# Attention of block 1 reordered: stick-breaking first, its mask by TensorE, up-projections by halves, selection rounds among the softmax heads

## What is computed

```python
(c_q, c_kv, k_rope, dq, dk, dv, iq, ik, iw, sq, sk, sv) = jnp.split(proj, offsets, axis=-1)
q = (rms_norm(c_q, mla_q_norm[i]) @ mla_w_uq[i])   # 6 MLA heads of 64 + 32 (rotary)
kv = (rms_norm(c_kv, mla_kv_norm[i]) @ mla_w_ukv[i])
s = einsum(mla_q, mla_k) * 96 ** -0.5; o_mla = softmax(where(causal, s)) @ mla_v
ilog = einsum(idx_q, idx_k) * IDX_DIM ** -0.5
isc = einsum(relu(ilog), idx_w)                    # 8 index heads, summed
_, sel = lax.top_k(isc, topk)                      # 64 of at most 256 keys per query
o_dsa = softmax(dsa_q @ kg + bias) @ vg            # 5 heads over the selected keys
z = einsum(sb_q, sb_k) * SB_DIM ** -0.5            # 5 stick-breaking heads
l1m = where(m, log_sigmoid(-z), 0); suffix = cumsum(l1m, reverse=True) - l1m
w = where(m, exp(log_sigmoid(z) + suffix), 0); o_sb = w @ sb_v      # m: strictly causal
h = h + concatenate([o_mla, o_dsa, o_sb]) @ w_o[i]
```

## Time and profile before

| | us |
|---|---|
| runs | 1634.23, 1616.0, 1617.82 (median 1617.82) |
| the profiled execution | 1622.2, its span 1620.4 |
| TensorE busy | 1470.7 (91%) |
| VectorE busy | 912.0 (56%) |
| ScalarE busy | 679.5 (42%) |
| GpSimd busy | 155.1 (10%) |
| chain that ended last | PE 79%, DVE 13%, issue 3%, ACT 3% |
| attention of block 1, layer 0 (27.9 to 208.4) | 180.5 |
| attention of block 1, layer 1 (457.6 to 619.3) | 161.7 |

### The profile page before, as it was taken

How to read it: one execution, slowest core, us unless ns; L and a number is a source line. 1 busy time by engine, 2 the same in 40 slices (tenths; PEclk the granted TensorE clock), 3 DMA queues, 4 the chain that set the end, 5 groups by cost and what they waited for, 6 DMA issues and landing times.

```text
span 1620.4 us, 24381 instructions
## 1 busy us (share of the span) xinstructions
PE 1470.7 (91%) x10258; PEld 1379.2 (85%) x10258; DVE 912.0 (56%) x1244; ACT 679.5 (42%) x957; POOL 155.1 (10%) x146
## 2 busy tenths in 40 slices
PE   7987999999889699999998959899999469899998
PEld 6977999999889689999986748899998458799997
DVE  5475355555656656555567563554565557365554
ACT  4442254334544435443356333344454224244442
POOL 2000010000110011000022100201021100010000
PEclk9996799999999899999999978899999579799999
DMA  8620145555453134555444431355545210045652
GB/s 233 181 104 1 59 147 192 191 176 183 126 153 143 53 112 162 190 183 196 174 142 154 153 109 53 130 172 192 175 164 189 104 52 2 1 152 186 197 174 98
DMA packets 159656, 225.09 MB, mean 139 GB/s; under 512 B 20105, under 2 KB 126601, under 8 KB 159548
## 3 DMA queue, kind: packets, MB, share of 16 engines
q1 hardware_dynamic: 159548, 223.55, 41.7%
HBM read 222.44 MB, written 1.09 MB: 138 GB/s over the span
## 4 chain that ended last, share of the span: by engine, by line
PE 79%; DVE 13%; issue 3%; ACT 3%; POOL 1%; DMA 0%; DVEq 0%; ACTq 0%; SPq 0%; POOLq 0%
PE ps L1932 16%; PE ps L1933 15%; PE ps L1934 15%; PE ps L1924 4%; PE ps L1925 4%; PE ps L1926 4%; DVE w_lo L1155 3%; PE ps L2162 3%; DVE xT L1179 3%; PE ps L2211 2%; PE ps L2212 2%; PE ps L2213 2%; PE ps L2172 2%; ACT w_hi L710 2%; DVE h L1194 1%
## 5 line engine op out<-in xcount | busy, mean ns | idle before, releaser
L1155 DVE TENSOR_TENSOR w_lo<-raw,w_hi 128x2048 fp32r<-128x2048 f32 (+4 forms) x209 | 476.9, 2288 | 294.1 <-ACT w_hi L710 291.5
L710 ACT ACTIVATE w_hi<-raw 128x2048 fp32r<-128x2048 f32 (+4 forms) x209 | 391.9, 1879 | 233.4 <-PE ps L1934 117.0
L1932 PE MATMUL ps<-xT,w_hi 128*128 128x256 f32 x1600 | 460.0, 287 | 14.9 <-DVE w_lo L1155 13.7
L1933 PE MATMUL ps<-xT,w_hi 128*128 128x256 f32 x1600 | 457.1, 286 | 0.0
L1934 PE MATMUL ps<-xT,w_lo 128*128 128x256 f32 x1600 | 456.9, 286 | 0.0
L1932 PEld LDWEIGHTS ps<-xT,w_hi 128*128 128x128 f32 x1600 | 311.9, 195 | 17.4 <-DVE w_lo L1155 14.9
L1933 PEld LDWEIGHTS ps<-xT,w_hi 128*128 128x128 f32 x1600 | 311.6, 195 | 0.6
L1934 PEld LDWEIGHTS ps<-xT,w_lo 128*128 128x128 f32 x1600 | 311.6, 195 | 0.0
L1932 PE MATMUL ps<-hT,w_hi 128*128 128x256 f32 x640 | 182.3, 285 | 4.6 <-DVE hT L1569 4.6
L1933 PE MATMUL ps<-hT,w_hi 128*128 128x256 f32 x640 | 182.1, 284 | 0.0
L1934 PE MATMUL ps<-hT,w_lo 128*128 128x256 f32 x640 | 182.0, 284 | 0.0
(11 more groups left out here) (290 smaller groups left out, 2097.9 us busy)
## 6 DMA issues: line engine op xcount, KB each, us to landing
raw<-in_w_up_dram SPq DMA_DIRECT2D x54, 1024.0 KB, 5.4
raw<-in_w_down_dram SPq DMA_DIRECT2D x54, 1024.0 KB, 4.9
raw<-in_w_gate_dram SPq DMA_DIRECT2D x22, 1024.0 KB, 5.2
raw<-in_w_in_dram SPq DMA_DIRECT2D x14, 1024.0 KB, 5.8
raw<-in_a_w_in_dram SPq DMA_DIRECT2D x10, 1024.0 KB, 5.1
raw<-in_w_o_dram SPq DMA_DIRECT2D x8, 1024.0 KB, 4.8
raw<-in_w_ple_gate_dram SPq DMA_DIRECT2D x8, 1024.0 KB, 4.8
raw<-in_w_out_dram SPq DMA_DIRECT2D x8, 1024.0 KB, 4.8
```

The lines of the kernel that those rows point to most:

```text
L710: nc.scalar.activation(w_hi[:, p % RH, 0:piece_width(p)], raw[:, p % RR, 0:piece_width(p)], ACT.Copy).then_inc(E["hi_ready"], 1)
L1155: nc.vector.tensor_tensor(w_lo[:, p % RH, 0:w], raw[:, p % RR, 0:w], w_hi[:, p % RH, 0:w].bitcast(F32), ALU.subtract).then_inc(E["lo_ready ...
L1932: nc.tensor.matmul(out_, w[0][:, kk, c], x(0, k), start=start and j == 0, stop=False, skip_group_check=True)
L1933: nc.tensor.matmul(out_, w[0][:, kk, c], x(1, k), start=False, stop=False, skip_group_check=True)
```

## The change

- The pieces come as tok, sq, sk, s4, iq, ikdk, cq, ckv, uq, ukv, dq, w_o; the four pieces of w_o in the order 3, 0, 1, 2 (`W_O`), and the ring's places follow.
- Stick-breaking's first scores lie between the blocks of iq, its second scores between later blocks, each followed by an index score. The index scores go to ps6 and ps7, their relu to `Tsel`.
- The mask is added by TensorE: ScalarE copies the mask and the unit matrix into a place of the ring, and each `stick_z` has two more matmuls of 128x128 (L2356, L2357), 20 in a layer. `stick_sums` and one multiplication on VectorE are gone; ScalarE takes the exponential from PSUM.
- The up-projections go by halves (`lora_half`), each into its own pair of banks.
- Of the eight selection rounds, two follow the stick-breaking outputs, two more stand just ahead of the heads, and one stands in each of the first four heads.
- The heads are a function of their own, with one bank for scores (ps0), one for transposes (ps2) and one for outputs (ps3). The outputs are transposed in pairs of blocks (`turned_pair`, L2547, to ps1): stick-breaking's ahead of the heads, one before head 7's scores, one before the last head is finished, one inside the output product, which starts behind the last values.

```diff
-        add(("w_o", l), tall("w_o", l, KD))
+        add(("w_o", l), [sub("w_o", l, 2 * i, 2, (0, D)) for i in W_O])
...
             def stick_logs(i):
                 dve.wait_ge(E["sb_r"], n["B"] + SB_H)
                 dve.wait_ge(E["sb_l"], n["B"] + i + 1)
-                link(nc.vector.tensor_tensor(sbN[i], sbN[i], sbL[i], ALU.add))
-                nc.vector.tensor_tensor(sbN[i], sbN[i], negm, ALU.mult).then_inc(E["sb_nl"], 1)
-
-            def stick_sums(i):
-                dve.wait_ge(E["sb_s"], n["B"] + i + 1)
-                nc.vector.scalar_tensor_tensor(sbL[i], PS[i % 2][:, 0:384], HD ** -0.5, smask,
-                                               op0=ALU.mult, op1=ALU.add).then_inc(E["sb_w"], 1)
+                nc.vector.scalar_tensor_tensor(sbN[i], sbL[i], -HD ** 0.5, sbN[i], op0=ALU.mult, op1=ALU.add
+                                               ).then_inc(E["sb_nl"], 1)
...
-                select(5 if l == 0 else 4)
-                selected()
-                outputs([MIX_SB + HD * a for a in range(4)], n["O"], None)
-                outputs([MIX_SB + HD * 4], n["O"] + 4, None)
...
+                index_mask()
+                outputs([MIX_SB + HD * a for a in range(4)], n["O"], None, bank=1)
+                outputs([MIX_SB + HD * 4], n["O"] + 4, None, bank=0)
                 cat(l, 1)
...
+                select(2)
+                rest_pair(6)
+                cat(l, 3)
+                used(("dq", l))
+                two_along(allT[:, B_DQ:B_DQ + 2, :], 4)
+                cat(l, 5)
+                select(2)
+                logits(0)
+                for i in range(4):
+                    logits(i + 1)
+                    select(1)
+                    move_pT(i)
+                selected()
...
-            def stick_z(i):
+            def stick_z(l, i):
...
+                mask, ident_r = mask_at(l)
+                nc.tensor.matmul(bank[:, 0:S], allT[r, k, 0:P], allT[r, q, :], start=True, stop=False, skip_group_check=True)
+                nc.tensor.matmul(bank[:, S:384], allT[r, k, P:S], allT[r, q, P:S], start=False, stop=False,
+                                 skip_group_check=True)
+                nc.tensor.matmul(bank[:, 0:P], ident_r, mask, start=False, stop=True, skip_group_check=True)
+                return nc.tensor.matmul(bank[:, S:384], ident_r, mask, start=False, stop=True, skip_group_check=True)
...
                 p = at("dq")
                 pe.wait_ge(E["lo_ready"], p + 1)
+                pe.wait_ge(E["ukv_a"], 2 * l + 1)
+                pe.wait_ge(E["ukv_d"], 2 * l + 1)
+                row_block(p, x, PS[4], 0, 0)
                 pe.wait_ge(E["rope_ready"], l + 1)
+                pe.wait_ge(E["ix_r"], n["X"])
                 cat(l, 0)
+                pe.wait_ge(E["ukv_a"], 2 * l + 2)
+                pe.wait_ge(E["ukv_d"], 2 * l + 2)
                 cat(l, 1)
...
+                pe.wait_ge(E["o_evac"], n["G"])
+                turned_pair(6)
+                row_block(p, x, PS[4], 1, P).then_inc(E["piece_used"], 1)
+                for c in range(2, len(CATS)):
+                    cat(l, c)
...
+                scores(0)
+                pe.wait_ge(E["rt_d"], 6 * l + 6)
+                for i in range(NJ):
+                    if i == 6:
+                        pe.wait_ge(E["o_evac"], G0 + 1)
+                        turned_pair(0)
+                    if i == NJ - 1:
+                        pe.wait_ge(E["o_evac"], G0 + 2)
+                        turned_pair(2)
+                    if i + 1 < NJ:
+                        scores(i + 1)
+                    transposes(i)
+                    if i:
+                        values(i - 1)
+                values(NJ - 1)
+                out_rows(0, 0, 2 * KD)
+                out_rows(1, 0, 2 * KD)
+                out_rows(2, 0, 9)
+                pe.wait_ge(E["o_evac"], G0 + 3)
+                turned_pair(4)
+                out_rows(2, 9, 2 * KD)
...
-                attention(mla_jobs() + dsa_jobs())
-                pe.wait_ge(E["o_evac"], n["G"])
-                to_T(KD, xs, wait_xs=False)
-                tall_product(("w_o", l), ("o", l), 4)
+                heads(l)
```

More of the change, by code:

```diff
@@ L88, in ffn_order @@
     return out + [down[-1]]
+W_O = (3, 0, 1, 2)
 def plan():
@@ L160, in place @@
 def place(use, k):
+    if use[0] == "o":
+        k = 2 * W_O.index(k // 2) + k % 2
     return (KD * USES.index(use) + k) % XR
@@ L496, in bass_two_blocks, with mask_at @@
         B_IQ, B_IK, B_DK, B_SQ, B_SK, B_S4, B_K4, B_DQ = 0, 4, 5, 6, 8, 10, 11, 12
-        CATS = [(src, dst, a) for src, dst in ((qcat, qT), (kcat, kT)) for a in range(0, MLA_H, 2)]
+        CATS = [(src, dst, a) for a in range(0, MLA_H, 2) for src, dst in ((qcat, qT), (kcat, kT))]
+        NJ = MLA_H + DSA_H
+        def mask_at(l):
+            two = xT[:, 0, place(("o", l), 2 * W_O[0]), :]
+            return two[:, 0:P], two[:, P:2 * P]
         def o_before(head0, i):
@@ L768, in mixing @@
                 m = NORM["attn", l] % 2
-                first, behind = FIRST["tok", l], FIRST["iq", l]
+                first, behind = FIRST["tok", l], FIRST["sq", l]
                 for p in range(first, behind):
@@ L1251, in wide_evac, with outputs @@
                     n["wide"] += 1
-            def outputs(dsts, J0, factor, gated=None):
+            def outputs(dsts, J0, factor, gated=None, bank=None):
                 G = n["G"]
@@ L2068, in lora_product @@
                     for t in range(NT):
-                        for half in range(2):
-                            i = by_tokens(PS[base + 2 * t + half][:, 0:w], hidden, k0 + k, t, ws, k, w * half,
-                                          w * half + w, k == 0, k == kn - 1)
-                i.then_inc(E["piece_used"], 1)
+                        i = by_tokens(PS[base + t][:, 0:w], hidden, k0 + k, t, ws, k, w * half, w * half + w,
+                                      k == 0, k == kn - 1)
+                return i
             def mlp(stage, name, blocks, gated):
@@ new lines, in mixing, with flip_ @@
+                pe.wait_ge(E["dkk_ready"], l + 1)
+                for t in range(NT):
+                    i = nc.tensor.transpose(PS[2][:, P * t:P * t + P], kdd[:, t, :], ident)
+                i.then_inc(E["dk_t"], 1)
+                row_block(p, x, PS[4], 0, P).then_inc(E["piece_used"], 1)
+                def flip_(j):
+                    if l == 0:
+                        if j:
+                            pe.wait_ge(E["toep_ready"], j)
+                        nc.tensor.matmul(PS[3][:, :], flip, Tdsa[:, 2 * j:2 * j + 2, :], start=True, stop=True
+                                         ).then_inc(E["flipped"], 1)
```

593 lines of the change are left out of this document (354 added, 239 removed).

## The result

The changed kernel took 1639.65 us (median of 17 runs, 1636.79 to 1677.08), the kernel before 1618.09 in the same comparison (17 runs, 1616.0 to 1638.35). The ratio is 1.010, with a 95% interval of 1.0069 to 1.0132: slower, by less than 2%. Forecast was 1624 in 1594 to 1640, so the time lies just inside the range, and about three times as far from the kernel before as forecast. The profiled execution has a span of 1636.2 us against 1620.4, 15.8 more.

What follows compares the result with a forecast made beforehand. TensorE bounds mixing, VectorE's chain the wait ahead of the heads, the clock the heads. At half clock layer 0 gives -6.2 and layer 1 +11.7, together +5.5 on 1617.8: 1623.3, say 1624 us; range 1594 to 1640.

Steps and rivals of the forecast that it cites:

- the zone: From the last index score to the first head's logits: VectorE chain of 22.9 us, TensorE idle 8.9 of it in pieces.
- D: Rival, mixing: mask products and changes between kinds of product at their upper ends, +9 us, 1633; chance 0.10.
- E: Rival, ahead of the heads: VectorE's chain only moves and nothing is saved, +15 us, 1639; chance 0.05.
- the +5.3: Mixing: TensorE work added per layer, in us, by overlap lost, mask matmuls and going between kinds of product.
- the lost overlap: Mixing: paired stick-breaking scores that ran together now run apart, three times 0.85, 2.6 us a layer.
- the changes of kind: Mixing: going between index-score and stick-breaking products and other blocks, some ten more places, 1.5 us a layer (0 to 3).
- the row block as nearest row: Mixing: a mask matmul priced from a row block's 128x256 matmul (0.12 to 0.13 us), taken as 0.07, upper end 0.22.
- -5.9: Layer 1, up to the end of the first logits: 564.9 instead of 570.8, 5.9 us earlier.
- 41.0: Heads, first logits to output product at half clock: 41.0 us, against 39.9 (layer 0) and 25.4 (layer 1) before.
- A: Rival, heads: full clock comes back or never falls in one layer; 1609, or 1617 if midway; chance 0.27.
- C: Rival, heads: single banks make one serial chain, 5.4 instead of 3.2 us a head, 1671 (over 1650); chance 0.04.
- B: Rival, heads: both layers at full clock, -23.5 us, 1594; chance 0.09.

Runs made afterwards that it cites:

- e8: The changed kernel without the 20 mask matmuls of a layer; 1633.22 us, one run.
- e5: The changed kernel with unused matmuls in TensorE's waits ahead of the heads and also within the heads; 1606.97 us, ratio to the kernel before 0.990.
- e11: e5 with two score banks and two transposed banks instead of one each; 1604.35 us, one run.
- e3: The changed kernel with two score banks and two transposed banks again, as in the kernel before; 1636.01 us, ratio to the kernel before 1.003.
- e2: The kernel before with unused matmuls (62 and 52) in TensorE's one long wait ahead of the heads; 1603.94 us, ratio 0.987.
- e7: e2 with unused matmuls also ahead of two places in mixing where stick-breaking's scores wait; 1598.87 us, ratio to the kernel before 0.985.
- e6: e1 with the four selection rounds moved from the first four heads to ahead of the first logits, 60 filling matmuls there; 1623.85 us, ratio 1.000.
- e1: The changed kernel with 26, 20 and 12 unused matmuls in three TensorE waits ahead of and within the first head; 1623.0 us, ratio to before 0.999.
- e9: e5 with three more unused matmuls ahead of each of four groups of the norms' one-column products in mixing; 1610.37 us, one run.
- e4: The changed kernel without the four selection rounds among the first four heads; 1634.71 us, ratio to the kernel before 1.008.
- e10: e7 with 9 more unused matmuls ahead of the turn and 34 ahead of layer 1's first mixing block; 1601.08 us, ratio to before 0.988.

## Why the prediction was right, and where it was off

**What bounds it** held: mixing is TensorE's, the zone VectorE's, the heads the clock's. The number held by little: 1639.65 against an upper end of 1640, with +5.5 us forecast and +15.8 in the traces. That it fell inside is luck, since the upper end was set by rivals D (1633) and E (1639), and what used that room was neither of them but the clock outside the heads.

**Mixing.** The last index score was to end at 113.1 and ended at 113.3 in layer 0. From the first block that is 86.0 us, not 85.2, so the +5.3 (its terms as written add to 5.5, 20 x 0.07 being 1.4) should have been 6.1 if the work before was 92.5, and its terms were off both ways: a mask matmul costs 0.135 us (e8), not 0.07, 2.7 a layer, and with 2.6 for the lost overlap some 0.8 are left for the changes of kind, not 1.5. The choice of the row block as nearest row was the weak one; between 0.06 and 0.22 the middle, 0.14, was true. No wait for stick-breaking's second scores is left.

**The wait zone.** In layer 0 the first logits were to end 108.1 us after the first block; they end 108.5 after it. The idle pieces were to be 0.4, 3.1, 2.9 and 2.5; they are 0.25, 3.45, 2.85 and 1.81. The chain added up from rows of VectorE came within a microsecond: 22.9 forecast, 22.6 measured.

**Layer 1's mixing is the step that failed.** -5.9 was forecast ahead of the logits, -1.5 measured. The chain of the zone is as long as in layer 0; of the 4.4 missing, 4.2 are clock:

```profile
451.60:457.80 6.20, 6.17 (x29) 6.17 (x30) 4.38 (x2) 0.00 (x0) 0.57 (x1) 0.50 0.85 270
517.00:522.70 5.70, 5.70 (x45) 5.46 (x43) 2.01 (x6) 0.11 (x1) 1.25 (x6) 1.00 0.48 187
522.70:529.50 6.80, 6.80 (x25) 5.93 (x25) 1.49 (x4) 1.69 (x4) 1.24 (x3) 0.50 0.00 0
```

The opening cost 3.1, not 2.3, and 6.8 us at half clock in the middle of mixing cost 3.4, with TensorE never idle in them or in the 5.70 us ahead. The working had taken the half-clock stretches of mixing before away with the waits and put nothing in their place. But the trace of the kernel before already had one that stands behind no wait, in layer 0:

```profile
68.00:73.20 5.20, 5.20 (x42) 4.89 (x41) 2.68 (x7) 2.02 (x2) 0.00 (x0) 1.00 0.45 151
73.20:76.60 3.40, 3.40 (x17) 3.40 (x17) 1.63 (x2) 0.00 (x0) 1.27 (x6) 0.50 0.20 23
```

**The heads.** 41.0 from first logits to product forecast, 41.3 measured in both layers (41.9 from the logits' start). Two of its terms were off and made up for each other: the output bank's two waits took 1.5 us, not 2.4, and VectorE's row made TensorE wait 2.3, not 1.5. The clock was at 0.50 in both, as taken. At full clock 28.0 was worked out for the changed heads; e5 measured 29.0, of which 1.6 is the single banks (e11).

**The product.** +2.0 a layer forecast, +2.2 and +3.3 measured; in layer 1 a second stretch at half clock lies in it (clock 0.92 against 1.00).

**Outside the change** nothing was forecast, and 4.0 us came. Its half-clock stretches are longer by 10 us in all, which would account for up to 5. Over all kernels of the table this unchanged rest takes 806.2 to 813.0 us. It was put at nothing without a reason given.

The sum: layer 0 -5.3 (-6.2 forecast), layer 1 +17.7 (+11.7), the rest +4.0 (0), and 0.6 us less before the first block: +15.8. The mechanism was right in the heads; the mis-sized term is the clock outside them: 4.2 ahead of layer 1's logits, 1.3 in its product and 4.0 in the rest, 9.5 of the 10.3 us that the forecast was short in the traces.

**The rivals.** A did not come by itself. C was excluded by e3. D was half true: the mask 2.7 instead of 1.3, the changes of kind, by the sum above, less. E did not come. B, both layers at full clock, was to give 1594. Made by filling, it gave layer 0 -21.6 (-20.7 worked out) and layer 1 +2.9 (-2.8), 1607 (e5). The forecast for B compared it with the kernel before at its own clock, and that is no fair comparison: filled too, the kernel before has 1604 (e2) and 1599 (e7).

**At equal clock, then, where did the gain go?** e7 against e5, without the half-clock stretches that each still has in this part (6.9 us in e7's layer 0, 6.8 in e5's layer 1, at half their length; the opening of layer 1 is in both): first logits at 110.7 and 108.6 in e7, at 107.9 and 107.3 in e5. So the new order does bring them forward, by 2.8 and 1.3 us. The heads give 3.7 and 4.0 back (29.0 against 25.3 and 25.0, and those have a short stretch at half clock at their turn): 4.6 for the rounds among the first four (e6), 1.6 for the single banks (e11). Splitting the rounds hides little when the clock is full, 1.2 of 5.8 us, since there VectorE bounds the first four heads, and adding the mask takes 4 us of the engine that bounds mixing. In the traces e5 is 7.9 us behind e7, and only 3.6 of that lie in the two layers' attention; 4.1 are in the unchanged rest, which the new order need not have caused. Without the mask products (e8) and with two banks (e11) it might come out ahead; the two together were not run.

**The clock and its rules.** With the long waits ahead of the heads filled, the half clock behind them was gone (e2: 40.6 to 25.3 us in layer 0). The Trainium skill, "TensorE: Matmul & The Clock Gate", section "HAM oscillation", says that waits between bursts of work drop the clock again and that the cost is paid anew each time; for these waits the traces agree. In e1 the clock also fell with waits of only 1.10 and 1.08 us, inside a stretch where TensorE was busy 2.68 of 4.90 us; the waits of the page's example are longer. In e6 layer 1's heads, three of whose thirteen products are transposes, ran 21.8 us at a clock of 1.00 with nothing added among them, and in the kernel before layer 1's clock came back amid such heads, at 574.9. The same page's Part 4, that the full clock does not engage for transposes, is therefore no rule for heads in which transposes are mixed with other products; what does hold is that the changed kernel's heads, once at half, never got the full clock back in 41.9 us, busy as TensorE was (38.98).

What stays open: why the clock falls in mixing with TensorE busy (the norms' one-column products stood a few us ahead of the fall at 73.2 before and at 522.7 after, but mixing them with filling in e9 did not keep the clock), why layer 1's heads regained it before the change and neither layer's after, and whether the longer runs of the kernel before, 1632 to 1642 us, are those in which layer 1's heads stay at half clock too. The 15 us of e2's layer 0 would fit, but none of those runs has a trace. If so, the change's loss against them would be 2 us (1638.2 against their median of 1636.4).

## What to carry to other kernels

Before moving work behind a wait of TensorE, ask what the clock does there: fill the wait with unused matmuls and time both kernels so; the gain of a reordering can be judged only at the same clock, and the filling itself may be the larger gain (0.985 here). Here one long wait was filled with one edit, and the same idle time in short pieces among real work took several. VectorE's work that is hidden behind TensorE at half clock may not be at full clock (0.6 us seen of 5.8 in e4, 4.6 by e6): work the sum out at both.

## What was not expected of the hardware

- A stretch of products can hold the full clock and yet not regain it: the heads of the changed kernel stayed at 0.50 for 41.9 us with TensorE busy 38.98, and those of e6's layer 1, the same products, stayed at 1.00 for 21.8 us.
- TensorE's clock fell to half at 522.7 with the engine busy 5.70 of the 5.70 us ahead, and in the kernel before at 73.2 with 5.20 of 5.20.
- Unchanged code takes 806.2 to 813.0 us over these traces; with one half-clock stretch taken away, others appeared (e10).
